# Three weight units at once at the start of a normed stage

## What is computed

```python
def first_block(...):
    h = rmsnorm(x, norm_mix_pre);  y = parallel_mixer(h, ...)          # convolution and attention
    x = x + rmsnorm(y, norm_mix_post)
    h = rmsnorm(x, norm_mem_pre);  y = memory_cross_attention(h, ...)  # 256 memory rows, 4 heads
    x = x + rmsnorm(y, norm_mem_post)
    h = rmsnorm(x, norm_ffn_pre);  y = conv_gated_ffn(h, ...)          # 2 x 2816 wide
    x = x + rmsnorm(y, norm_ffn_post)

def second_block(...):
    for i in range(2):
        x = x + 0.5 * swiglu(rmsnorm_2(x, ffn1_norm[i]), ...)
        x = x + (pool_mixer, then mla_mixer)(rmsnorm_2(x, mix_norm[i]), ...)
        x = x + 0.5 * swiglu(rmsnorm_2(x, ffn2_norm[i]), ...)
```

## Time and profile before

| | us |
|---|---|
| median of 3 runs (2616.62 to 2622.31) | 2621.32 |
| the profiled execution | 2623.71 |
| its span | 2622.4 |
| TensorE busy | 2566.9 |
| VectorE busy | 1225.3 |
| ScalarE busy | 934.4 |
| GpSimd busy | 620.9 |

### The profile page before, as it was taken

One profiled execution on the slowest core, in us unless ns is written; L12 is line 12 of the kernel. 1 busy time (PEld: TensorE's weight loads), 2 busy tenths in 40 slices (PEclk: granted clock), 3 DMA queues, 4 the chain that ended last, 5 costly groups with the idle time before them and its releaser, 6 DMA issues.

```text
span 2622.4 us, 28823 instructions
## 1 busy us (share of the span) xinstructions
PE 2566.9 (98%) x11706; PEld 2097.2 (80%) x11706; DVE 1225.3 (47%) x1613; ACT 934.4 (36%) x1372; POOL 620.9 (24%) x471
## 2 busy tenths in 40 slices
PE   9898999999999999999999999999999999999999
PEld 7766777788887888888888888888788787888887
DVE  6896665555525333335333333333336565533322
ACT  4485343444423333224333222333223454333321
POOL 3663302222203222101222101222001431222200
PEclk9999999999999999999999999999999999999999
DMA  4211312333232233232333232333332111333232
GB/s 167 67 46 41 104 49 65 97 97 97 91 97 78 89 97 96 91 95 77 105 96 97 90 94 89 97 97 94 97 102 66 47 43 39 98 97 96 95 97 90
DMA packets 66484, 227.28 MB, mean 87 GB/s; under 512 B 7216, under 2 KB 8752, under 8 KB 66352
## 3 DMA queue, kind: packets, MB, share of 16 engines
q1 hardware_dynamic: 66352, 225.44, 27.4%
HBM read 223.31 MB, written 2.10 MB: 86 GB/s over the span
## 4 chain that ended last, share of the span: by engine, by line
PE 89%; DVE 6%; ACT 2%; issue 2%; POOL 0%; DMA 0%; SPq 0%; DVEq 0%; ACTq 0%; POOLq 0%
PE main L380 20%; PE main L381 19%; PE main L382 19%; PE score L380 7%; PE score L381 6%; PE score L382 6%; PE out L380 3%; PE out L381 3%; PE out L382 3%; DVE wl L372 1%; DVE cv L626 1%; PE main L1997 1%; PE turn L450 1%; PE turn L449 1%; DVE tmp L1313 1%
## 5 line engine op out<-in xcount | busy, mean ns | idle before, releaser
L372 DVE TENSOR_TENSOR wl<-raw,wh 128x1024 fp32r<-128x1024 f32 (+1 forms) x431 | 561.5, 1305 | 816.9 <-ACT wh L364 816.4
L364 ACT ACTIVATE wh<-raw 128x1024 fp32r<-128x1024 f32 (+1 forms) x431 | 440.3, 1025 | 612.4 <-PE main L382 503.5
L380 PE MATMUL main<-hxh,wh 128*128 128x512 f32 x1208 | 476.1, 394 | 8.6 <-DVE wl L372 3.3
L382 PE MATMUL main<-hxh,wl 128*128 128x512 f32 x1208 | 472.7, 391 | 0.0
L381 PE MATMUL main<-hxl,wh 128*128 128x512 f32 x1208 | 472.5, 391 | 0.0
L380 PE MATMUL main<-hh,wh 128*128 128x512 f32 x880 | 347.8, 395 | 1.5 <-DVE tmp L1604 0.8
L382 PE MATMUL main<-hh,wl 128*128 128x512 f32 x880 | 347.5, 395 | 0.0
L381 PE MATMUL main<-hl,wh 128*128 128x512 f32 x880 | 347.5, 395 | 0.0
L380 PEld LDWEIGHTS main<-hxh,wh 128*128 128x128 f32 x1208 | 228.1, 189 | 62.3 <-issue 8.1
L438 POOL TENSOR_TENSOR acc<-acc,sq 128x512 f32<-128x512 f32 (+1 forms) x84 | 120.1, 1430 | 648.8 <-ACT sq L433 643.9
L380 PE MATMUL score<-hxh,wh 128*128 128x512 f32 x664 | 261.2, 393 | 6.5 <-DVE wl L372 4.8
(11 more groups left out here) (403 smaller groups left out, 3457.5 us busy)
## 6 DMA issues: line engine op xcount, KB each, us to landing
raw<-in_wts SPq DMA_DIRECT2D x375, 512.0 KB, 3.5
raw<-in_wts SPq DMA_DIRECT2D x52, 384.0 KB, 3.1
x<-in_xT SPq DMA_DIRECT2D x4, 512.0 KB, 7.2
out<-x SPq DMA_DIRECT2D x8, 256.0 KB, 3.9
memx<-in_memT SPq DMA_DIRECT2D x1, 1024.0 KB, 9.3
raw<-in_wts SPq DMA_DIRECT2D x4, 256.0 KB, 2.6
band<-in_pool SPq DMA_DIRECT2D x1, 768.0 KB, 4.5
rope<-in_rope SPq DMA_DIRECT2D x1, 512.0 KB, 6.8
```

Of the source, the lines that this page charges most:

```text
L364: e.activation(wh[i % NCONV][:, 0:n], raw[i % NRAW][:, 0:n], ACT.Copy).then_inc(*sig.up("weight_high", ("high", i)))
L372: e.tensor_tensor(wl[i % NCONV][:, 0:n], raw[i % NRAW][:, 0:n], f(wh[i % NCONV][:, 0:n]), ALU.subtract) \
L380: e.matmul(o, ah, bh, start=start, stop=False)
L382: return e.matmul(o, al, bh, start=False, stop=stop)
```

## The change

A new `linear_three` takes three units through the parts: two as before, and the third two parts behind. The memory stage, the FFN and f10 begin with it. The sums then follow unit 3, not unit 2, and the rows' transpose unit 4, not unit 3. So that unit 2 is there in time, its high and low halves are made earlier: in the norm ahead of the FFN and f10, the high half before the splits and the low half between the mean square and the first part; in the norm ahead of the memory stage, inside the loop over the parts (high before part 4, low behind part 6). Nothing is added or taken away; the queues of GpSimd and SyncE are the same.

```diff
+        def linear_three(e, i, o0, o1, o2, src):
+
+            for k in range(KC):
+                pair_step(e, i, o0, o1, src, k)
+                if k > 1:
+                    unit_step(e, i + 2, o2, src, k - 2)
+            for k in range(KC - 2, KC):
+                unit_step(e, i + 2, o2, src, k)
...
+            if not fillers:
+                high(e, end + 3)
...
+                if fillers and m == 4:
+                    high(e, U_MQ + 2)
...
-            if fillers:
-                low(e, U_VAL[1][1] + 2)
+            low(e, U_VAL[1][1] + 2 if fillers else u + parts * KC + 2)
...
+                if fillers and m == 6:
+                    low(e, U_MQ + 2)
...
-            linear_pair(e, U_MQ, query_banks.of(("mq", 0))[:, :], query_banks.of(("mq", 1))[:, :], normed("mem"))
-            for m in range(2, KC):
+            linear_three(e, U_MQ, *(query_banks.of(("mq", m))[:, :] for m in range(3)), normed("mem"))
+            for m in range(3, KC):
...
-                if m == 2:
+                if m == 3:
                     square_sums(e, "mem", KC - 1)
-                if m == 3:
+                if m == 4:
                     spread_rows(e, "mem", ("root", "mem"))
...
-                if n == 1:
-                    linear_pair(e, U_UP, wide.of(("tile", 0))[:, :], b[:, :], normed("ffn"))
-                elif n > 1:
+                if n == 2:
+                    linear_three(e, U_UP, *(wide.of(("tile", i))[:, :] for i in range(3)), normed("ffn"))
+                elif n > 2:
                     linear(e, U_UP + n, b[:, :], normed("ffn"))
-                    if n == 2:
+                    if n == 3:
                         square_sums(e, "ffn", KC - 1)
-                    if n == 3:
+                    if n == 4:
                         spread_rows(e, "ffn", ("root", "ffn"))
...
+                elif c == 1 and nm in LATE:
+                    linear_three(e, u, wide.of((nm, "gate", 0))[:, :], wide.of((nm, "up", 0))[:, :], g[:, :], normed(nm))
+                    linear(e, u + 3, p[:, :], normed(nm))
+                    square_sums(e, nm, KC - 1)
+                elif c > 0:
                     linear(e, u + 2 * c, g[:, :], normed(nm))
-                    if c == 1 and nm in LATE:
-                        square_sums(e, nm, KC - 1)
-                    elif c == 1:
+                    if c == (2 if nm in LATE else 1):
                         spread_rows(e, nm, ("root", nm))
```

More of the change, by code:

```diff
@@ L405, in pair_step, with unit_step @@
                     made.then_inc(*sig.up("unit_done", ("unit", i + n)))
+        def unit_step(e, i, o, src, k):
+            sh, sl, ready = src(k)
+            e.wait_ge(*sig.at(ready))
+            h, lo = weights_of(i)
+            e.wait_ge(*sig.at(("low", i)))
+            made = mm3(e, o, (h[:, k, :], lo[:, k, :]), (sh, sl), k == 0, k == KC - 1)
+            if k == KC - 1:
+                made.then_inc(*sig.up("unit_done", ("unit", i)))
+        def linear_three(e, i, o0, o1, o2, src):
[5 more added lines that the diff above has]
+                unit_step(e, i + 2, o2, src, k)
         def linear_pair(e, i, o0, o1, src):
@@ L1345, in memory_tensor @@
         def memory_tensor(e):
-            for m in range(2):
+            for m in range(3):
                 _, old = query_banks.take(("mq", m))
                 e.wait_ge(*sig.at(old))
-            linear_pair(e, U_MQ, query_banks.of(("mq", 0))[:, :], query_banks.of(("mq", 1))[:, :], normed("mem"))
-            for m in range(2, KC):
+            linear_three(e, U_MQ, *(query_banks.of(("mq", m))[:, :] for m in range(3)), normed("mem"))
+            for m in range(3, KC):
                 b, old = query_banks.take(("mq", m))
@@ L1564, in swiglu_tensor @@
                 e.wait_ge(*sig.at(old_g))
-                if c == 0:
+                if c < 2:
                     e.wait_ge(*sig.at(old_p))
+                if c == 0 and nm not in LATE:
                     linear_pair(e, u, g[:, :], p[:, :], normed(nm))
-                    if nm not in LATE:
-                        square_sums(e, nm, KC - 1)
-                else:
+                    square_sums(e, nm, KC - 1)
+                elif c == 1 and nm in LATE:
+                    linear_three(e, u, wide.of((nm, "gate", 0))[:, :], wide.of((nm, "up", 0))[:, :], g[:, :], normed(nm))
+                    linear(e, u + 3, p[:, :], normed(nm))
+                    square_sums(e, nm, KC - 1)
+                elif c > 0:
                     linear(e, u + 2 * c, g[:, :], normed(nm))
-                    if c == 1 and nm in LATE:
-                        square_sums(e, nm, KC - 1)
-                    elif c == 1:
+                    if c == (2 if nm in LATE else 1):
                         spread_rows(e, nm, ("root", nm))
@@ L1577, in swiglu_tensor @@
                     linear(e, u + 2 * c + 1, p[:, :], normed(nm))
-                    if c == 1 and nm in LATE:
-                        spread_rows(e, nm, ("root", nm))
             for m in range(KC):
```

## The result

| | before | after |
|---|---|---|
| median of 5 runs each (us) | 2620.44 (2616.62 to 2622.31) | 2631.21 (2628.06 to 2634.01) |
| the profiled execution | 2623.71 | 2631.21 |
| its span | 2622.4 | 2629.9 |

The ratio is 1.0043, with an interval of 1.0032 to 1.0054: 0.43% or 10.8 us slower, which is more than the 0.2% that a measurement tells from no change. The forecast was 2627.5, 0.24% slower; both its sign and its range (2618 to 2633) held, its size was 4 us short.

The account below looks back on a forecast made before the run. TensorE, busy 98% of the span, was taken as the bound. Memory +4.55, FFN -0.25 and f10 +1.9 us, clock losses included, made +6.2 on a median of 2621.3: 2627.5 us, range 2618 to 2633.

Parts of the forecast that it names:

- The gaps, and sums without a wait: FFN, f10: nine matmuls per part gain 3.1 us per stage; the 1.26 us wait before the sums and its clock loss go.
- Unit 3's wait: FFN: unit 3, run before the sums, waits about 0.6 us for its low half.
- rival C: New waits with clock losses, and the clock also lost after the sums in the three stages: +11 us, 2632.3; chance 0.1.
- E: Rival: unit 2's weights late for its first group, waiting 0.5 to 1 us in one stage: +2 to +5; chance 0.15.
- The inverse root: Before FFN and f10: GpSimd's root beside VectorE's low half slows, so everything after comes 0.91 us later in two stages.
- What stood behind the rows: Weights queued behind the rows come a unit late: new waits of 4.55 us (memory), 2.85 (FFN), 4.9 (f10).
- Rival D: Late weights do not stop TensorE, so no new waits or clock losses in the three stages: -10.9 us, 2610.4; chance 0.1.
- The clock behind the waits: Clock lost behind each of the three new waits: 1.6 us each, bounds 0 and 4.8 together.
- FFN and f10: Net stage changes including the clock: FFN -0.25 us, f10 +1.9 us.
- The sum: Memory, FFN and f10 together, with three new waits and clock losses: +6.2 us, 2627.5; chance 0.45.
- Rival B: The three new waits come but the clock holds behind them: +1.4 us, 2622.7; chance 0.2.

Follow-up runs that it names:

- e6: e1 plus unit 2's low half moved ahead of the mean square in the norms before the FFN and f10; 2611.4 us, 0.9967 of the kernel before.
- e7: Kernel before with only unit 2's earlier conversion in the norms ahead of the FFN and f10; 2620.01 us against 2618.58, ratio 1.0006.
- e1: Changed kernel with the late weight conversions moved ahead of the rows in the ScalarE and VectorE queues, all three stages; 2614.58 us against 2621.04 before, 0.9975.
- e5: e6 with the memory stage as before the change, except high halves of its units 5 and 6 ahead of the row copy; 2610.11 us against 2618.58 before, 0.9968.
- e8: e6 with the low halves of units 1 and 2 one part earlier in the memory stage; 2610.15 us against 2618.58 for the kernel before, 0.9964.
- e10: Changed kernel with sums back behind unit 2 and transpose behind unit 3, three units at once kept; 2621.06 us against 2621.22 before, 0.9999.
- e2: Changed kernel with idle matmuls filling the waits behind the transposes (memory, FFN) and behind unit 5 (f10); 2623.49 us against 2621.04 before, 1.0004.
- e3: Kernel before with the change in the memory stage alone; 2627.41 us against 2621.04, ratio 1.0022.
- e9: The changed kernel measured once more, word for word; 2630.17 us against 2621.22 for the kernel before, ratio 1.0033.
- e4: Changed kernel with the memory stage as before, so the change in FFN and f10 alone; 2622.03 us, 1.0004 of the kernel before.

## Why the prediction was right, and where it was short

- **The gaps, and sums without a wait: right.** From the FFN's first matmul to the sums it is 23.10 us (460.61 to 483.71); the working gave 23.2. Unit 3's wait was put at 0.6 and is 0.26 (FFN; 0.16 in f10): smaller, without effect. All three sums have a clock of 1.00, so rival C falls. The premise that sums without a gap keep the clock was read from too few sets: the kernel before has one near 2027 that breaks it (last part). It held in the three stages. Unit 2 was not late, so E falls.
- **The inverse root: right**, 1.93 us, and e6 shows 0.9 per stage. As a price by itself it was wrong (e7): in the order before, the shorter adds gave it back.
- **What stood behind the rows: right.** Forecast 4.55, 2.85 and 4.9, measured 4.43, 2.60 and 4.97 in each profile that has them. This is the step that turns a gain into a loss. Rival D falls: the waits are there. Its price for a kernel without them, -10.9 us, is built by e1, which is 6.5 us below before in the medians and 7.6 in the stages. The FFN (-4.4) and f10 (-4.6) are near D's -4.7 and -4.6; the memory stage is +1.3 where D has -1.6, and in e1 its attention ran at half clock. The 2610 of e5 and e8 is reached only with the inverse root freed as well.
- **The clock behind the waits: right in kind, mis-sized in the memory stage.** The transposes and unit 5 stand where they were forecast: from unit 1's wait to unit 5 it is 35.40 us against 32.64 before, +2.8 for a forecast of +2.95. Then 1.6 was added for the clock. The windows show 3.4 x 0.50 + 3.4 x 0.29 = 2.7, and the rest, 7.98 - 2.8 - 2.7 = 2.5 us, is where the attention runs at half clock. That loss was in no term; the forecast said the attention moves along unchanged. It does not hang on the wait alone: of the eight profiles with three units in the memory stage, four have it (the change, e1, e6, e10), three of them without the wait; e2, e3, e8 and e9 don't, nor do the four with the old order. What sets it off stays open. e9 has neither excess and gives +4.50 for a forecast of +4.55, e3 +5.3. So the clock cost between 1.4 and 5.2 us here from one profile to the next, and I had taken a value near the lower end, 1.6, both as the cost and as its upper bound.
- **FFN and f10:** forecast -0.25 and +1.9; measured -0.31 and +2.54, in e9 -1.83 and +2.11. The FFN differs by just the clock loss of 1.6 (3.4 x 0.47) behind its 2.60 us wait, which is there in one profile of three.
- **The sum:** +6.2 forecast. The stages give +10.2 and +4.8 in two profiles of the kernel; the medians +10.8 and +9.0. Between +7.5, the mean of the two profiles' stages, and the medians some 2 us remain that I can't place: code that didn't change varies by 6 to 7 us between profiles. The granted clock over the whole span gives a hint: its mean is 0.984 and 0.985 in the two sets of five runs of the change, and 0.987 in the 32 and 17 runs of the kernel before on the chips of e1 and e9. The forecast had no such fall, since it set three new losses against the three behind the sums. So the change has more time at low clock than the forecast gave it (some of it inside the waits, where it costs nothing); which stretches take it in the runs without a profile stays open. The single effects of e3 (+6.4) and e4 (+1.0) sum to +7.4, a little under the whole, within the intervals.
- **Rival B**, that the clock holds, is what e2 builds: 2623.5 for its 2622.7. It falls for the change itself, but its price was right.

## What to carry to other kernels

When a synchronizing step (here the rows' transpose) moves a unit later on one engine, list what stands behind its result in the in-order queues of the other engines: those steps move with it, and whatever the old order hid is now waited for. Filling gaps of the engine that bounds the kernel gained here only where the next thing it waits for (the adds of squares) was not already late, and only with the queues mended to the new order: +9 to +11 us became -6 by moving some conversions ahead of the rows, and -7 to -9 with unit 2's low half ahead of the mean as well. Where a wait can't be removed, idle matmuls in it are worth a try: in e2 they kept the clock behind all three.

## What the runs showed of the hardware

- **A short wait ahead of the sums mostly costs the clock.** The sums are 16 tiny matmuls. Over the twelve profiles, 36 sets of them have a wait of 0.22 to 3.5 us ahead; behind 30 the clock fell within 3 us. It held behind 6: one with 1.25 us in e3 (f10, where the FFN's 1.26 lost it), and five of the twelve with 0.73 us at f10's output norm (the change, e3, e4, e6, e9). Without a wait the sums of the three stages always kept it, but this is no rule. One set later in the kernel has no wait and is followed by eight more tiny matmuls, and the clock fell behind it in all twelve profiles. In the kernel before, the nearest long wait is one of 2.27 us, 4 us ahead of it. Timeline and window of that kernel:

```profile
2027.54 0.38 PE L449 MATMUL turn<-ones,acc 128*128 128x1 f32 x2
...
2029.34 1.03 PE L1997 MATMUL main<-ones,sq 128*128 128x1 f32 x8
...
2031.00:2034.40 3.40, 3.40 (x10) 2.59 (x9) 3.35 (x7) 0.00 (x0) 2.25 (x2) 0.52 0.00 0
```

- **The clock behind waits in dense work.** The six waits of 4.43 and 4.97 us with large matmuls behind them all cost the clock or a part of it, the one of 2.60 in one profile of three. One loss cost 1.4 to 2.7 us. The Trainium skill (TensorE: Matmul & The Clock Gate, section HAM oscillation) describes the clock lost to idle time between bursts. For the long waits e2 against the change agrees. The sums lost it behind a far shorter wait than those that it describes (0.63 behind 0.22 us), and there the measurement decides.
- **VectorE's low half delays GpSimd even on a tiny operation.** Four numbers a partition take GpSimd 1.02 us alone and 1.93 beside a low half of 1.22; six adds take 11.55 us with three low halves beside them and 10.74 with two. The Trainium skill (SBUF — State Buffer, section SBUF: two separate sides) describes a port pair that the one that starts first holds for its whole instruction. The order in time agrees: the low half starts at 453.49, the root at 453.66, and their ends are 454.71 and 455.59, so the root has 0.9 us to itself after it.
